# Gate matmuls of a recurrent layer in three split passes, with the splits on ScalarE and VectorE

## What is computed

```python
def rg_lru(u, w_r, b_r, w_i, b_i, lam, reverse):
    ub = u.reshape(bsz, s, LRU_BLOCKS, LRU_BLOCK_DIM)          # 16 blocks of 128
    gate_r = jax.nn.sigmoid(jnp.einsum('bsni,nij->bsnj', ub, w_r)... + b_r)
    gate_i = jax.nn.sigmoid(jnp.einsum('bsni,nij->bsnj', ub, w_i)... + b_i)
    log_a = -LRU_C * gate_r * jax.nn.softplus(-lam)
    a = jnp.exp(log_a)
    in_scale = jnp.sqrt(-jnp.expm1(2.0 * log_a))
    b = in_scale * (gate_i * u)
    _, h = lax.associative_scan(_linear_combine, (a, b), axis=1, reverse=reverse)
    return h
...
u = centred_depthwise_conv(u_lru, conv_w[l], conv_b[l])
h = rg_lru(u, ..., False) + rg_lru(u, ..., True)
y_a = h * jax.nn.silu(g_lru)
```

## Time and profile before

| | |
|---|---|
| median of 3 runs | 3135.65 us |
| the profiled execution, first to last instruction | 3131.3 us |
| TensorE busy | 3053.0 us, 97% |
| VectorE busy | 1787.8 us, 57% |
| ScalarE busy | 1469.7 us, 47% |
| mean granted TensorE clock | 0.993 |
| gate matmuls, L1692 | 128 records, first 2600.9 us, last 2846.3 us |

### The profile page before, as it was taken

How to read it: one execution, slowest core, us unless ns; L and a number is a source line. 1 busy time by engine, 2 the same in 40 slices (tenths; PEclk the granted TensorE clock), 3 DMA queues, 4 the chain that set the end, 5 groups by cost and what they waited for, 6 DMA issues and landing times.

```text
span 3131.3 us, 37290 instructions
## 1 busy us (share of the span) xinstructions
PE 3053.0 (97%) x13980; PEld 2525.8 (81%) x13980; DVE 1787.8 (57%) x2323; ACT 1469.7 (47%) x1956; POOL 49.3 (2%) x77
## 2 busy tenths in 40 slices
PE   8999999999999999969999999999999999999998
PEld 6877888888888787758888888888888888777886
DVE  6535554545455777845554545455545557886554
ACT  6434444444444445434444434344444456786333
POOL 0000000000000000000000000000000000110000
PEclk9999999999999999989999999999999999999999
DMA  7545565555655564425566565655665555666664
GB/s 261 179 131 186 188 191 188 188 188 188 188 188 181 169 193 136 128 67 181 191 193 188 189 188 188 188 188 186 218 194 178 178 164 173 192 204 208 215 242 148
DMA packets 294504, 574.06 MB, mean 183 GB/s; under 512 B 18128, under 2 KB 30800, under 8 KB 293584
## 3 DMA queue, kind: packets, MB, share of 16 engines
q1 hardware_dynamic: 286720, 541.13, 54.1%
q0 software_dynamic: 7056, 29.63, 2.8%
q10 hardware_dynamic: 576, 1.20, 0.1%
HBM read 561.41 MB, written 10.49 MB: 183 GB/s over the span
## 4 chain that ended last, share of the span: by engine, by line
PE 88%; DVE 6%; ACT 4%; issue 2%; DMA 0%; DVEq 0%; ACTq 0%
PE acc L1530 27%; PE acc L1532 27%; PE acc L1531 27%; PE tp L1543 2%; DVE wlo L1031 2%; ACT whi L776 1%; ACT prob L951 1%; PE sd L1644 1%; PE sd L1678 0%; PE sd L1611 0%; PE sd L1617 0%; ACT qk L959 0%; DVE set_lo L1129 0%; ACT L951 0%; PE sd L1668 0%
## 5 line engine op out<-in xcount | busy, mean ns | idle before, releaser
L1530 PE MATMUL acc<-whi,set_hi 128*128 128x512 f32 x4096 | 1623.7, 396 | 26.1 <-DVE wlo L1031 16.5
L1532 PE MATMUL acc<-whi,set_lo 128*128 128x512 f32 x4096 | 1600.1, 391 | 0.0
L1531 PE MATMUL acc<-wlo,set_hi 128*128 128x512 f32 x4096 | 1598.8, 390 | 0.0
L1031 DVE TENSOR_TENSOR wlo<-raw,whi 128x1024 fp32r<-128x1024 f32 x1024 | 1226.4, 1222 | 623.4 <-ACT whi L776 621.6
L776 ACT ACTIVATE whi<-raw 128x1024 fp32r<-128x1024 f32 x1024 | 1051.7, 1057 | 653.3 <-PE acc L1532 622.4
L1530 PEld LDWEIGHTS acc<-whi,set_hi 128*128 128x128 f32 x4096 | 771.8, 188 | 198.9 <-DVE wlo L1031 29.4
L1532 PEld LDWEIGHTS acc<-whi,set_lo 128*128 128x128 f32 x4096 | 771.0, 188 | 162.6
L1531 PEld LDWEIGHTS acc<-wlo,set_hi 128*128 128x128 f32 x4096 | 772.1, 188 | 154.6
L1125 DVE TENSOR_TENSOR set_lo<-tp,set_hi 128x1024 fp32r<-128x1024 f32 x36 | 44.1, 1225 | 181.4 <-ACT set_hi L875 181.4
L875 ACT ACTIVATE set_hi<-tp 128x1024 fp32r<-128x1024 f32 x36 | 36.9, 1026 | 188.6 <-PE tp L1543 188.6
L1063 DVE TENSOR_TENSOR stage_b<-stage_a 128x1024 f32<-128x1024 f32 x32 | 39.2, 1226 | 142.2 <-ACT stage_a L823 142.2
(11 more groups left out here) (210 smaller groups left out, 1158.3 us busy)
## 6 DMA issues: line engine op xcount, KB each, us to landing
raw<-in_w_ff SPq DMA_DIRECT2D x512, 512.0 KB, 4.4
raw<-in_w_in SPq DMA_DIRECT2D x272, 512.0 KB, 4.3
raw<-in_w_out SPq DMA_DIRECT2D x96, 512.0 KB, 4.5
raw<-in_w_mem_kv SPq DMA_DIRECT2D x32, 512.0 KB, 4.4
raw<-in_w_proj_a SPq DMA_DIRECT2D x32, 512.0 KB, 4.3
raw<-in_w_proj_b SPq DMA_DIRECT2D x32, 512.0 KB, 5.3
raw<-in_w_kv SPq DMA_DIRECT2D x48, 256.0 KB, 3.1
raw<-in_w_kv SPq DMA_DIRECT2D x24, 512.0 KB, 3.8
```

The lines of the kernel that those rows point to most:

```text
L1031: V.tensor_tensor(wlo[:, c], raw[:, c], whi[:, c].bitcast(f32), ALU.subtract).then_inc(w_lo, 1)
L1530: T.matmul(o, h[:, tok], whi[:, c], start=first, stop=False)
L1531: T.matmul(o, h[:, tok], wlo[:, c], start=False, stop=False)
L1532: ins = T.matmul(o, l[:, tok], whi[:, c], start=False, stop=last)
```

## The change

The gate products are made like the slab products, in three fp32r passes instead of one float32 product. ScalarE gets a new step `gate_split` at slab p-1, which stands behind `gates` of the block before: it copies the 512 columns of gate weights into `gw_hi` and the 256 columns of `xhs` into `gx_hi`. VectorE gets a step of the same name at slab p-1, behind `conv`: `gw_lo = lw - gw_hi` and `gx_lo = xhs - gx_hi`. The four tiles lie in `mkv`. There is one copy of them, so ScalarE waits for the gate matmuls of the block before. TensorE issues 12 matmuls of 256 columns for a block instead of 4. The wait of `lru_w` for the place in `lw`, and the first `merge_load`'s wait for `mkv`, are adapted.

```diff
         sc.at("dve", p - 1, "conv", n)
+        sc.at("act", p - 1, "gate_split", n)
+        sc.at("dve", p - 1, "gate_split", n)
         sc.at("pe", p, "gates", n)
...
+        gw_hi, gw_lo, gx_hi, gx_lo = (
+            nc.alloc_sbuf_tensor_at(name, [P, cols], f32r, offset=place["mkv"][0] + 4 * first)
+            for name, first, cols in (("gw_hi", 0, 4 * P), ("gw_lo", 4 * P, 4 * P), ("gx_hi", 8 * P, TOK),
+                                      ("gx_lo", 8 * P + TOK, TOK)))
...
             def merge_load(i, a):
                 pool.wait_ge(sm["mg_out"], 128)
                 if i == 0:
-                    pool.wait_ge(sm["att_lo"], row_jobs(NJOB))
+                    pool.wait_ge(sm["gates_pe"], LB)
...
             def lru_w(n):
                 if n >= 2:
-                    pool.wait_ge(sm["gates_pe"], at(n - 1))
+                    pool.wait_ge(sm["gate_lo"], n - 1)
...
+            def gate_split(n):      # ScalarE
+                act.wait_ge(sm["att_lo"], row_jobs(NJOB))
+                act.wait_ge(sm[f"lw{n % 2}_in"], at(32 * (n // 2 + 1)))
+                if n:
+                    act.wait_ge(sm["gates_pe"], n)
+                A_(gw_hi[:], lw[:, (n % 2) * 4 * P:(n % 2 + 1) * 4 * P], ACT.Copy).then_inc(sm["gate_w"], 1)
+                act.wait_ge(sm["conv_ok"], n + 1)
+                A_(gx_hi[:], xhs[:, TOK * (n % 2):TOK * (n % 2 + 1)], ACT.Copy).then_inc(sm["gate_hi"], 1)
...
+            def gate_split(n):      # VectorE
+                dve.wait_ge(sm["gate_w"], n + 1)
+                V.tensor_tensor(gw_lo[:], lw[:, (n % 2) * 4 * P:(n % 2 + 1) * 4 * P], gw_hi[:].bitcast(f32),
+                                ALU.subtract)
+                dve.wait_ge(sm["gate_hi"], n + 1)
+                V.tensor_tensor(gx_lo[:], xhs[:, TOK * (n % 2):TOK * (n % 2 + 1)], gx_hi[:].bitcast(f32),
+                                ALU.subtract).then_inc(sm["gate_lo"], 1)
...
             def gates(n):           # TensorE
-                pe.wait_ge(sm["conv_ok"], at(n + 1))
+                pe.wait_ge(sm["gate_lo"], n + 1)
                 if n:
                     pe.wait_ge(sm["gates_ok"], at(n))
                 pe.wait_ge(sm["att_lo"], row_jobs(NJOB))
-                pe.wait_ge(sm[f"lw{n % 2}_in"], at(32 * (n // 2 + 1)))
-                for d in range(2):
-                    for k in range(2):
-                        o = 2 * d + k
-                        w = lw[:, ((n % 2) * 4 + o) * P:((n % 2) * 4 + o + 1) * P]
-                        ins = T.matmul(sd[:, TOK * o:TOK * (o + 1)], w, xhs[:, TOK * (n % 2):TOK * (n % 2 + 1)],
-                                       start=True, stop=True)
+                for o in range(4):
+                    to = sd[:, TOK * o:TOK * (o + 1)]
+                    w = slice(P * o, P * (o + 1))
+                    T.matmul(to, gw_hi[:, w], gx_hi[:], start=True, stop=False)
+                    T.matmul(to, gw_hi[:, w], gx_lo[:], start=False, stop=False)
+                    ins = T.matmul(to, gw_lo[:, w], gx_hi[:], start=False, stop=True)
                 ins.then_inc(sm["gates_pe"], 1)
```

More of the change, by code:

```diff
@@ L527, in build @@
                  "pool_mix", "pool_mid", "pool_mm", "pool_hi", "pool_lo",
-                 "conv_ok", "gates_pe", "gates_ok", "lru_sq", "lru_root", "lru_ok",
+                 "conv_ok", "gate_w", "gate_hi", "gate_lo", "gates_pe", "gates_ok", "lru_sq", "lru_root", "lru_ok",
                  "lru_hi", "lru_lo", "lruc_ok", "lexp_ok",
@@ L982, in _ @@
                          pool_mid=pool_mid, pool_hi=pool_hi,
-                         gates=gates, root=root, lru_hi=lru_hi, epi_add=None, epi_proj_a=None, epi_proj_b=None)
+                         gate_split=gate_split, gates=gates, root=root, lru_hi=lru_hi, epi_add=None, epi_proj_a=None, epi_proj_b=None)
             def run(slab):
@@ L1467, in _ @@
                          rope2=rope2, att_smx=att_smx, att_prob=att_prob, att_o=att_o, att_lo=att_lo,
-                         pool_lo=pool_lo, lru_const=lru_const, conv=conv,
+                         pool_lo=pool_lo, lru_const=lru_const, conv=conv, gate_split=gate_split,
                          lru_square=lru_square, lru=lru, lru_lo=lru_lo,
```

## The result

The kernel before takes 3134.99 us (median of five executions, 3134.2 to 3135.89), the changed kernel 3147.09 us (five, 3147.04 to 3148.93). That is 12.1 us more; the ratio is 1.0042 with an interval of 1.0031 to 1.0053. The forecast was 3149.3 us and its range 3143 to 3158: 2.2 us too high, and right in sign and inside the range.

The account below looks back on a forecast made before the run. A closed ScalarE-VectorE loop bounds the recurrence, TensorE following. Copies 13.05 us plus late convolutions 0.9, less 0.35 for the first gate product, give +13.6; 3131.3 + 13.6 + 4.35 = 3149.3 us, range 3143 to 3158.

Parts of the forecast that it names:

- The step from the waits to a closed loop: In the recurrence ScalarE and VectorE wait only for each other, 16.29 us a turn; TensorE needs 15.36 and follows.
- rival (1): Idle time of ScalarE and VectorE absorbs both steps, TensorE is the bound: 5.6 us less, 3130.0 us; chance 0.10.
- ScalarE's copies: Two copies in slab a, ahead of slab b's split, add 0.87 us a turn, 15 x 0.87 = 13.05 us.
- Late convolutions: Where VectorE's convolution ends after `gates`, gx_hi waits: 0.63 us extra in block 2, some 0.15 in 5 and 13; 0.9 in all.
- VectorE's subtractions at nothing: 0.94 us a block, covered by VectorE's 2.50 us idle time before slab b's subtraction, so costed at nothing.
- Rival (3): VectorE's cover fails and its 0.94 us a block join the path: 28 us more, 3163 us; chance 0.07.
- TensorE's passes: Gate product takes 1.4 us instead of 1.73; only the first block's counts on the path, -0.35 us.
- rival (4): Passes take 2.7 us a block, only the first showing, +1.0 instead of -0.35: 3150.6 us; included in the 0.80 chance.
- The clock: TensorE's granted clock may fall in every plain period of the recurrence, costing 1.7 us, within its 2.1 us of idle time.
- rival (2): Clock falls cost 3.4 us each, exceeding TensorE's idle time by 1.3 a period: 33 us more, 3169 us; chance 0.03.
- The last fall: Clock fall at TensorE's last stall, 2859.36 us in the kernel before; without it TensorE ends up to 1.7 us earlier.
- the 4.35 us "around the span": Median of runs minus the profiled span of 3131.3 us, taken as time around the span and added to the forecast.

Follow-up runs that it names:

- the third copy: Changed kernel with one more ScalarE copy of 512 columns a block, gate weights into a spare place, ahead of the two: 3154.4 us.
- VectorE's part alone: Kernel before with VectorE's two subtractions a block added, each operand from itself; no ScalarE copies, float32 products: 3137.2 us.
- the first experiment: Changed kernel with both gate_split steps kept for block 0 only, TensorE still making the 12 passes for all 16 blocks: 3134.85 us.
- the last kernel: Changed kernel with all four split operations moved into waits, lru_hi one slab later and the Tanh table load ahead of its wait: 3119.83 us.
- the kernel with `lru_hi` later: Changed kernel with ScalarE's lru_hi moved one slab later, behind the split of slab a: 3134.75 us.
- the one with the table load early: Changed kernel with lru_hi one slab later and a four-column Tanh ahead of its wait to bring the table load: 3123.02 us.
- the same edits without splits: Kernel before, float32 gate products, with lru_hi one slab later and a four-column Tanh ahead of its wait: 3123.73 us.

## Why the prediction was right, and where it was off

**What bounds the kernel.** The step from the waits to a closed loop held. The two gate products that frame a turn with no epilogue in slab a or b start 2842.14 - 2825.02 = 17.12 us apart on TensorE's timeline of the changed kernel, forecast 17.2:

```profile
2825.02 0.28 PE L1713 MATMUL sd<-gx_hi,gw_hi 128*128 128x256 f32 x1
...
2842.14 0.28 PE L1713 MATMUL sd<-gx_hi,gw_hi 128*128 128x256 f32 x1
```

That the loop sets the pace, and not only that it looks so, is shown by work of the same size at other places: in the loop a copy is paid in full (the third copy, +7.3 us, and 7.0 expected), in waits the four splits together cost 2.0 us of 13.4 between the landmarks, and +0.8 us in the median, which is within the measurement. This is against rival (1), 3130.0 us, which let the idle time absorb both steps; it would have needed that idle time to lie where the copies were put.

**ScalarE's copies.** 0.83 us instead of 0.87: the term is 15 x 0.83 = 12.45 us and not 13.05. Reading the hold of an operation as the distance to the next start, from rows of like width, came within 5%.

**Late convolutions.** 13.39 - 12.45 = 0.94 us, forecast 0.9. The turns show that this is no accident of a difference: beyond 0.83 us, block 2 cost 0.69 (forecast 0.63), blocks 5 and 13 cost 0.16 and 0.14 (forecast 0.15 each), and the others nothing. Block 2 on ScalarE's timeline:

```profile
2628.09 0.61 ACT L953 ACTIVATE gw_hi<-kv 128x512 fp32r<-128x512 f32 x1
2629.78 0.42 ACT L955 ACTIVATE gx_hi<-ob 128x256 fp32r<-128x256 f32 x1 [1.08 <-DVE ob L1372]
2630.11 1.99 ACT L782 ACTIVATE whi<-raw 128x1024 fp32r<-128x1024 f32 x2
```

Here the pair takes 2630.11 - 2628.09 = 2.02 us, with 1.08 us of recorded wait in it. That is 0.50 us more than the 1.52 us by which the turn grew. In the kernel before, VectorE was late for slab b in this turn by as much: its subtraction started 2626.98 - 2625.40 = 1.58 us behind ScalarE's split, where a plain turn has 1.08.

**VectorE's subtractions at nothing.** Held in the plain turns: 2.06 us idle before `gw_lo` (forecast 2.1) and 0.23 before slab b (0.3). Rival (3), 3163 us, falls with this and with the experiment on VectorE's part alone. That experiment also shows the limit of the cover: alone the subtractions cost 2.55 us between the landmarks, in four turns with a late convolution. In the changed kernel the copies delay slab b in the same turns, so the two parts don't add up: 13.55 + 2.55 = 16.10 us, and 13.39 measured. Beside the copies VectorE's part costs nothing.

**TensorE's passes.** 0.119 us apart (forecast 0.114), 12 in 1.43 us, against 1.73 for the single product: 0.30 less instead of 0.35, so rival (4), 2.7 us a block, falls. That the fifteen others don't count here, and do once TensorE is the bound, is shown by the first experiment and by the last. The 0.30 us of the first gate product rest on the starts in two profiled executions alone; the times are too coarse for it.

**The clock.** The stall rows and the clock (seventh column of a stretch's numbers, ahead of the DMA share) of the changed kernel:

```profile
2650.20 0.50 PE L1553 MATMUL acc<-whi,set_hi 128*128 128x512 f32 x1 [2.38 <-DVE wlo L1046]
...
2720.21 0.50 PE L1553 MATMUL acc<-whi,set_hi 128*128 128x512 f32 x1 [2.47 <-DVE wlo L1046]
...
2738.49 0.50 PE L1553 MATMUL acc<-whi,set_hi 128*128 128x512 f32 x1 [2.92 <-DVE wlo L1046]
...
2874.60 0.50 PE L1553 MATMUL acc<-whi,set_hi 128*128 128x512 f32 x1 [2.11 <-DVE wlo L1046]
```

```profile
2650.00:2654.00 4.00, 3.80 (x10) 3.05 (x11) 3.93 (x8) 3.97 (x6) 0.43 (x1) 0.61 0.68 197
2720.00:2724.00 4.00, 3.79 (x20) 3.29 (x21) 3.45 (x7) 2.96 (x4) 0.44 (x1) 1.00 0.69 197
2738.00:2742.00 4.00, 3.51 (x10) 2.79 (x11) 3.97 (x7) 2.34 (x4) 1.98 (x3) 0.70 0.62 185
2872.00:2880.00 8.00, 5.18 (x22) 3.65 (x21) 6.14 (x9) 6.04 (x7) 0.56 (x1) 1.00 0.43 148
```

Of 15 stalls two brought the fall from 2.4 to 1.2 GHz, those at 2650 and 2738 us; the one of 2.47 us between them did not, and neither did that of 2.11 us at 2874.60, 14.6 us behind the last gate product, where the kernel before had its fall. The loop's pace shows neither of the two falls: they lie in the turns of blocks 3 and 8, which grew by 0.84 and 0.81 us like the rest. So rival (2), 3169 us, falls. The last fall, which didn't happen, was not worth the 1.7 us that the low end of the range allowed for it either: from `lru_hi` of block 15 to the end of the span it was 263.66 us and is 263.42. The Trainium skill, "TensorE: Matmul & The Clock Gate", section "HAM oscillation — how this bites in real kernels", has each wait of its loop bring a fall, but those waits are longer than any stall here (2.92 us at most). My step from it to 15 falls went beyond the page, and this trace has two falls in 15 stalls, none of them on the path.

**What was off.** The forecast amounts to the median of before that I had, 3135.65 us, and 13.6 us. Of the 2.2 us that it is too high, 0.7 are that median (with five executions it is 3134.99), and 0.5 are the sum: with the measured terms it is -0.30 + 12.45 + 0.94 = 13.1 us, where the copies are the term that was mis-sized. The last 1.0 us is 13.1 against the measured 12.1, less than the interval of the two medians. One step was wrongly named: the 4.35 us "around the span". In the changed kernel that quantity is 3148.07 - 3146.3 = 1.77 us, and 1.8 in its four other executions. In the kernel before it is 1.8 to 2.2 us, 2.0 in the middle, in the 57 executions beside the experiments. So some 2.3 us of the 4.35 were that the profiled execution was shorter than the median one, which goes with the 2.15 us by which the two profiles differ ahead of the change. And 0.2 or 0.3 us of the missing 1.0 lie outside the span, in this quantity, for which the forecast had no term; the rest stays open. The upper end of the range, 3158 us, doesn't come out of its words (half of the way from 3155 to 3163 is 3159), and nothing hangs on it.

**Where my later expectations missed.** Three expectations missed: the kernel with `lru_hi` later gained 12.3 us and not 15 or more, the one with the table load early came out at 3123.0 and not 3118, and it is not 5 us ahead of the same edits without splits but 0.7. In the first two I took the loop to be shorter by all that an edit moved, and both times the convolution, queued on VectorE behind two slab subtractions, was late next (`gx_hi` waited for it 2.8 and 2.1 us in four blocks, and each such wait delays slab b). With the splits in the waits as well, the last kernel gained 15.3 us where the one with both edits on the changed kernel gained 11.6. So 3.7 of the 5 us that were missing hung on where the splits stand, 4.33 between the landmarks (250.63 and 246.30), and the third miss is the same. What the rest is made of was argued only.

## What to carry to other kernels

Before an operation is priced at nothing because its engine is idle, look for who does not wait for whom: two engines that wait only for each other are a loop, and there an operation costs what it holds its engine for, however idle both are on average. Then the same operation can be moved into one of the loop's waits, as soon as its own inputs are there, and costs nothing in each turn that has such a wait; count the turns that don't. A faster TensorE pays only once that loop is shorter than TensorE's own turn.

## What the hardware showed that I had not expected

- A pass of 256 columns follows the one before it after 0.119 us with a new weight load each time, although each is recorded with 0.28 us; the recorded durations of twelve add up to 3.4 us, in 1.43 us of time. Only starts can be used for such passes.
- A stall of 2.38 us brought a clock fall and one of 2.47 us none. In the kernel before it fell after one of 1.79 us. The length of TensorE's stall alone doesn't tell whether the clock falls.
- A change of activation table holds ScalarE for little more than the recorded 1.28 us of the load: in the changed kernel the load starts at 2748.15 and the Tanh at 2749.45, 1.30 us later.
